# Neighbourhood attention: the product with the values as one fp32 product instead of three fp32r products

## Chip, cores and metric

The kernel runs on one core of one Trainium2 chip. The metric is the time of one execution on the device in microseconds (us). Three runs of the kernel before gave 3692.43 us as their median, with 3691.71 and 3695.13 as their ends.

## The reference

The program is a two-layer backbone over 1024 latent tokens with 256 context tokens. The second layer runs a latent attention (C) and beside it a two-dimensional neighbourhood attention (D). The change touches only D: 8 heads of width 64, the latents seen as 16 rows of 64 columns. A query sees 8 rows of keys around its own and in each of them 16 columns around its own column, with a learned bias, and all 256 context tokens.

```
def row_block(args):
    r, qr = args
    rs = jnp.clip(r - kr // 2, 0, rows - kr)
    krows = lax.dynamic_slice_in_dim(kg, rs, kr, axis=1).reshape(B, kr * GRID_W, H, d)
    ...
    kk = jnp.concatenate([krows, kc], axis=1)
    vv = jnp.concatenate([vrows, vc], axis=1)
    return mha_attend(qr, kk, vv, bias, mask)

def mha_attend(q, k, v, bias=None, mask=None):
    ...
    p = jax.nn.softmax(s, axis=-1)
    return jnp.einsum('bhqk,bkhd->bqhd', p.astype(v.dtype), v)
```

All of it is float32. The last line, exponentials times values, is what is computed in another way.

## The kernel before

`trunk` issues the stages one after the other, each a block of five instruction streams with its own semaphores. `attend` (L1855) is one function for three stages: "ab" (window attention, layer 0, 405 to 601 us of the trace), "ac" (latent attention, layer 1) and "ad" (neighbourhood attention, layer 1, about 2605 to 2846 us). After "ad" comes `layer_end`, which reads what "ad" stored.

Tiling. A query tile is 128 tokens and so is a key tile. Four query tiles are a block. `steps_of_head` lists for one head, block by block, the key tiles that any query tile of the block sees: 16 steps a head. A step works on one key tile and the 1 to 4 neighbouring query tiles that see it, so it is 128 to 512 columns wide. The widths of a head's steps are, in order: 512 (context), 384, 512, 512, 512, 256, 128, 512 (context), and for the second block 512 (context), 128, 256, 512, 512, 512, 384, 512 (context). Two heads make a pair of 32 steps, and `walk` runs four pairs, the middle ones in a loop.

One step x, engine by engine:
- TensorE (PE), `score` (L2111): keys times queries into one of three PSUM banks (L2129), bias added as two products with the identity (L2131), the row of maxima brought in by a last product of 65 rows (L2134, which waits for `row` on a block's first step).
- ScalarE (ACT), `exps` (L2211): with `split`, the exponential twice, once as float32 (`pt_sb`, L2217) and once rounded to fp32r (`ph`, L2218); without, once (L2220).
- VectorE (DVE), `low_part` (L2327): `pl` = `pt_sb` - `ph` (L2331), only with `split`.
- PE, `values` (L2136): the product with the values of an earlier step, x - LAG, accumulated over a block into one PSUM bank (L2151).
- At a block's end ACT copies the sums (`take_sums`, L2222) at the step LAG after the block's last, PE transposes them (`turn`, L2155) at the step after that, and DVE divides by the total (`result`, L2305). The first product with values of the next block waits for that copy.

Once a head, with `split`, ACT makes `vh` from the values (L2203) and DVE `vl` (L2325). Between the steps PE also computes rough scores for the coming block (`rough`, L2086: L2097 and L2100), DVE takes their maxima (L2293) and builds a diagonal of them (L2297), and PE spreads these over all rows (`extreme`, L2103: L2108), from which ACT makes the row (`extreme_row`, L2194: L2199). SyncE (SP) loads the next pair's queries, keys and values in `fetch` (L2040), after `s.pv` says that the last product of that head and pair is done (L2047).

The order on each engine is fixed by x alone. Two numbers of it hang on `split`:

```
PT, LAG = 4, 3 if split else 2
...
if split:
    pe.wait_ge(s.lo, nth(i, x))
    ...
else:
    pe.wait_ge(s.ex, nth(i, x))
...
prods = ((vh, ph), (vl, ph), (vh, pl)) if split else ((v_sb, pt_sb),)
for y, (v, e) in enumerate(prods):
    mm = pe.matmul(k.ps[0:v_width + 1, OB, (t.q - q0) * P:(t.q - q0 + t.n) * P], v[:, p, t.key],
                   e[:, x % PT, 0:t.n * P], start=(t.first and y == 0), stop=(t.last and y == len(prods) - 1))
```

The stage "ab" is called with `split` false; "ac" and "ad" with `split` true. The arrays `v_sb` and `pt_sb` are float32, the four split ones fp32r.

Of the kernel before, what the change touches and what calls it, by code (L numbers as in the profile page):

```python
# [33 lines left out]
HD = 64  # L34
# [210 lines left out]
def next_free(nc):  # L245

    return -(-nc.sbuf_base // 32) * 32
# [1552 lines left out]
def window_pieces():  # L1800

    out = []
    for q in range(LT):
        lo, hi = max(0, q - 1), min(LT, q + 2)
        masks = ([(0, CTX)] if q > 0 else []) + ([(1, CTX + (q + 1 - lo) * P)] if q < LT - 1 else [])
        out.append(Piece(q, [(SEQ, CTX), (lo * P, (hi - lo) * P)], masks=masks))
    return out + [Piece(q, [(SEQ, CTX)]) for q in range(LT, NT)]


def neighbour_pieces():  # L1810

    out = []
    for q in range(LT):
        rows = [min(max(r - NA_ROWS // 2, 0), 2 * LT - NA_ROWS) for r in (2 * q, 2 * q + 1)]
        n = rows[1] - rows[0] + NA_ROWS
        n += n % 2

        out.append(Piece(q, [(SEQ, CTX), (rows[0] * GRID_W, n * GRID_W)],
                         bias=(rows[0] - 2 * q + NA_ROWS - 1, n, rows[1] > rows[0])))
    return out  # L1820
# [549 lines left out]
def stacked_loader(qk, q_base, k_index, v_dram, v_index, v_width, n_q):  # L2370

    def load(sp, i, p, places, near, far):
        if sp is None:
            return 3, 3
        q_sb, k_sb, v_sb, q_top, k_top = places
        h, kh, vh = i * 2 + p, k_index(i, p), v_index(i, p)
        if q_sb is not None:
            keys(sp, h, kh, q_sb, k_sb, q_top, k_top, near, far)
        if v_sb is not None:
            sp.dma_start(v_sb, v_dram.rearrange("(t p) d -> p t d", p=P)[:, :, bass.ds(vh * v_width, v_width)]).then_inc(far, 16)  # L2380

    def keys(sp, h, kh, q_sb, k_sb, q_top, k_top, near, far):
        one = lambda x: qk[bass.ds(x, 1)].squeeze(0)
        sp.dma_start(f32(q_sb[:, 0, 0:n_q]), one(h + q_base)[:, 0:n_q]).then_inc(near, 16)
        for half in range(2):
            sp.dma_start(f32(k_sb[half * HD:(half + 1) * HD, 0]), one(kh)[0:HD]).then_inc(near, 16)
        sp.dma_start(f32(q_top[:, 0:n_q]), one(h + q_base)[0:HD, 0:n_q]).then_inc(far, 16)
        sp.dma_start(f32(k_top), one(kh)[HD:2 * HD]).then_inc(far, 16)
    return load


def parts_loader(k):

    def load(sp, i, p, places, near, far):
        if sp is None:
            return 2, 3
        q_sb, k_sb, v_sb, _, _ = places
        h = i * 2 + p
        one = lambda x: k.qkC[bass.ds(x, 1)].squeeze(0)
        for part, sem in enumerate((near, far)):  # L2400
            sp.dma_start(f32(q_sb[0:MLA_QK, part, 0:SEQ]), one(h)[part, :, 0:SEQ]).then_inc(sem, 16)
            sp.dma_start(f32(k_sb[0:MLA_QK, part]), one(h + MLA_HEADS)[part]).then_inc(sem, 16)
        sp.dma_start(v_sb, k.vC.rearrange("(t p) d -> p t d", p=P)[:, :, bass.ds(h * MLA_V, MLA_V)]).then_inc(far, 16)
    return load


def bias_loader(k):


    def load(sp, i, p, place, placeT, sem):  # L2410
        first_row = (i * 2 + p) * RPB_R + 1
        for q in range(2):
            sp.dma_start(place[q * GRID_W:(q + 1) * GRID_W],
                         k.bias[:, bass.ds(first_row - q, 2 * NA_ROWS - 2)]).then_inc(sem, 16)
            for key in range(2):
                first = 1 + q - key
                rows = k.biasT[:, first:first + 2 * NA_ROWS - 2].rearrange("k (d two) h c -> k d two h c", two=2)[:, :, 0]
                sp.dma_start(placeT[key * GRID_W:(key + 1) * GRID_W, :, q * GRID_W:(q + 1) * GRID_W],
                             rows[:, :, bass.ds(i * 2 + p, 1)].squeeze(2)).then_inc(sem, 16)
    return load  # L2420
# [965 lines left out]
def trunk(nc, out, **ins):  # L3386
    with ExitStack() as st:
        k = Core(nc, st, ins, out)
        ev = ins["ev_w_in"][0]
        load_b = stacked_loader(k.qkB, 0, lambda i, p: 8 + i // 2, k.vB, lambda i, p: i // 2, HD, TOK)  # L3390
        load_d = stacked_loader(k.qkD, 0, lambda i, p: i * 2 + p + 8, k.vD, lambda i, p: i * 2 + p, HD, SEQ)
        ahead_b = HeadAhead(k, st, "hb", SBUF_END, load_b, ins["wtab"], sink=ins["swa_sink"][0])
        ahead_a = DiffAhead(k, st, "ha", ahead_b.end)
        rows_0, rows_1 = RowsAhead(k, st, "h0", 0, KT // 2), RowsAhead(k, st, "h1", 1, 0)
        ahead_d = HeadAhead(k, st, "hd", SBUF_END, load_d, ins["ntab"], bias=bias_loader(k))
        units_b = [Unit(512, 512, 8, ins["swa_q_g"][0], HD ** -0.5, True, k.qkB, 0),
                   Unit(1024, 256, 2, ins["swa_k_g"][0], 1.0, True, k.qkB, 8, v=128, v_dst=k.vB),
                   Unit(0, 512, v=512, v_dst=k.vA)]
        made_b = ProjectionAhead(k, "pb", 1280, units_b, 2)
        opening(k, ev, 1024, made_b)  # L3400
        start_a = ProjectionStart(k, st, "pa", 0, ev, 0, made_b.raw_at, made_b.h_at)
        stores_b = project(k, "pb", 0, ev, 1024, 1280, units_b, keeps_h=True, vectors=(2, 3), made=made_b, begins=start_a)
        stores_a = project(k, "pa", 0, ev, 0, 1024, [
            Unit(0, 512, 8, ins["diff_q_g"][0], HD ** -0.5, True, k.qkA, 0),
            Unit(512, 512, 8, ins["diff_k_g"][0], 1.0, True, k.qkA, 8)], keeps_h=False, ahead_of=ahead_b, vectors=(4, 5),
            begun=start_a, stores_before=stores_b)
        ahead_d.hold_biases(st, rows_1.offset)
        stores_ab = attend(k, "ab", window_pieces(), 8,
               load_b,
               "two", False, HD, k.mix[0], 512, sink=ins["swa_sink"][0], beside=BiasSpread(k, ins["na_rpb"][0]),  # L3410
               ahead=ahead_b, ahead_of=ahead_a, last_stores=stores_a[0], stores_before=stores_a[1], keys_of=ahead_a)
        o_at = next_free(k.nc) + 100 * 1024
        stores_aa = attend_diff(k, "aa", ins, ahead_a, rows_0, stores_ab, o_at)
        layer_end(k, "e0", 0, TOK, [(0, 512), (512, 512), (1024, 256)], ins["w_out"][0], ins["mlp_w1"][0], ins["mlp_w2"][0], rows_0, stores_aa,
                  subln=ins["diff_subln_g"][0], following=ins["ada_w"][1])
        od = ins["od_w_in"][0]
        weights_end = next_free(k.nc) + 8 * KT * 1536
        start_c = LowRankStart(k, st, "pc", 1, od, next_free(k.nc), weights_end, weights_end + 8 * RAW_SLOTS * 256 + 4 * KT * P)
        stores_d = project(k, "pd", 1, od, MLA_QL + MLA_KVL + MLA_ROPE, 1536, [
            Unit(0, 512, 8, ins["na_q_g"][0], HD ** -0.5, False, k.qkD, 0, latents=True),  # L3420
            Unit(512, 512, 8, ins["na_k_g"][0], 1.0, False, k.qkD, 8),
            Unit(1024, 512, v=512, v_dst=k.vD)], keeps_h=True, sums_at=NEXT_BANKS, begins=start_c)
        project_low_rank(k, "pc", 1, od,
            Rank(0, MLA_QL, 0, ins["mla_qa_g"][0], ins["mla_wq_up"][0], ins["mla_q_g"][0], MLA_QK ** -0.5, 0, False),
            Rank(MLA_QL, MLA_KVL, MLA_ROPE, ins["mla_kva_g"][0], ins["mla_wkv_up"][0], ins["mla_k_g"][0], 1.0,
                 MLA_HEADS, True), start_c, stores_d)
        stores_ac = attend(k, "ac", [Piece(q, [(0, TOK)]) for q in range(LT)], MLA_HEADS, parts_loader(k), "three", True, MLA_V, k.mix[1], 0,
                           ahead_of=ahead_d, builds=ahead_d)
        stores_ad = attend(k, "ad", neighbour_pieces(), NA_HEADS,
               load_d,  # L3430
               "two", True, HD, k.mix[1], 512, bias=bias_loader(k), ahead=ahead_d, rows_of=rows_1, stores_before=stores_ac,
               o_at=next_free(k.nc) + 84 * 1024)
        layer_end(k, "e1", 1, SEQ, [(0, 512), (512, 512)], ins["w_out"][1], ins["mlp_w1"][1], ins["mlp_w2"][1], rows_1, stores_ad)
        k.phases.end()
# [21 lines left out]
```

## Time and profile before

| | |
|---|---|
| median of three runs | 3692.43 us (3691.71 to 3695.13) |
| the profiled execution, its own time | 3693.51 us |
| its span, first to last instruction | 3691.7 us |
| TensorE busy | 94% of the span |
| VectorE busy | 59% |
| ScalarE busy | 36% |
| mean granted TensorE clock | 0.969 |

The profile is of one execution. A matmul's end is modelled, so a drawn record reaches into the next one; the distance between two starts is the pace. "PEld" is TensorE's loading of weights, which runs ahead of the products. The idle time of an engine that nothing waits for costs nothing.

### The profile page before, as it was taken

What the parts mean: (1) busy time and instruction counts of PE and PEld (TensorE: products, weight loads), DVE (VectorE), ACT (ScalarE), POOL (GpSimd) and SP (SyncE); (2) the same over time, 40 slices, a digit from 0 to 9 for tenths busy, and PEclk for the clock granted to TensorE, in tenths of its full rate; (3) what the DMA queues carried; (4) which work ended last, traced back from release to release, by engine and by line L of the source; (5) the groups of instructions that cost most, each with busy time, mean ns of one, the idle gap of its engine ahead of it and who ended that gap; (6) DMA issues with size and microseconds to landing.
All of it is one profiled execution on the core that took longest, in us unless ns stands there. A gap on an engine that the chain in (4) does not pass through costs nothing. (4 is left out here: it accounts for less than half of the span.)

```text
span 3691.7 us, 47952 instructions
## 1 busy us (share of the span) xinstructions
PE 3479.7 (94%) x17598; PEld 2838.9 (77%) x17598; DVE 2171.4 (59%) x3199; ACT 1333.0 (36%) x2429; POOL 190.8 (5%) x197
## 2 busy tenths in 40 slices
PE   7999898998999999999989997899999999999998
PEld 4878666886888888888868786676787778888887
DVE  5879666886755444554475554788686553333333
ACT  5543344664511111111145554566565421111111
POOL 1110300000300000000001001000000110000000
PEclk8999899999999999999989998899999999999999
DMA  6566565324322212222233544233454311111112
GB/s 237 196 223 215 133 136 137 78 57 133 92 73 65 65 52 71 67 69 61 62 119 129 196 141 135 61 72 88 85 113 96 109 40 52 50 47 51 51 46 69
DMA packets 433093, 366.45 MB, mean 99 GB/s; under 512 B 104469, under 2 KB 375077, under 8 KB 427813
## 3 DMA queue, kind: packets, MB, share of 16 engines
q1 hardware_dynamic: 432933, 364.36, 34.9%
q8 instruction: 96, 1.57, 0.2%
q14 instruction: 64, 0.52, 0.1%
HBM read 276.60 MB, written 87.69 MB: 99 GB/s over the span
## 5 line engine op out<-in xcount | busy, mean ns | idle before, releaser
L2687 DVE SCALAR_TENSOR_TENSOR xT<-ps,mods,xT 128x1024 f32<-128x1024 f32 (+1 forms) x190 | 187.8, 1016 | 352.5 <-PE ps L2928 352.5
L3287 DVE TENSOR_TENSOR e_plain<-e_plain 128x1280 f32<-128x1280 f32 (+1 forms) x64 | 86.9, 1358 | 482.2 <-ACT e_plain L3126 482.2
L2928 PE MATMUL ps<-e_gh,e_w2h 128*128 128x512 f32 x1280 | 352.1, 372 | 6.0 <-DVE e_w2l L3225 3.7
L2928 PE MATMUL ps<-e_gh,e_w2l 128*128 128x512 f32 x1280 | 349.1, 370 | 0.0
L2928 PE MATMUL ps<-e_gl,e_w2h 128*128 128x512 f32 x1280 | 349.0, 370 | 0.0
L3126 ACT ACTIVATE e_plain<-ps 128x1280 f32<-128x1280 f32 (+1 forms) x64 | 72.7, 1135 | 722.7 <-PE ps L2928 718.6
L2928 PE MATMUL ps<-e_hh,e_w1l 128*128 128x512 f32 (+1 forms) x1200 | 327.2, 370 | 0.0
L2928 PE MATMUL ps<-e_hl,e_w1h 128*128 128x512 f32 (+1 forms) x1200 | 327.2, 370 | 0.0
L2928 PE MATMUL ps<-e_hh,e_w1h 128*128 128x512 f32 (+1 forms) x1200 | 327.1, 370 | 0.0
L2928 PEld LDWEIGHTS ps<-e_gh,e_w2h 128*128 128x128 f32 x1280 | 222.4, 188 | 55.1 <-DVE e_gl L3291 8.0
L3074 ACT CAST e_w2h<-e_raw 128x512 fp32r<-128x512 f32 x128 | 79.3, 620 | 499.4 <-PE ps L2928 499.4
L2928 PEld LDWEIGHTS ps<-e_gh,e_w2l 128*128 128x128 f32 x1280 | 223.5, 188 | 42.9
L2928 PEld LDWEIGHTS ps<-e_gl,e_w2h 128*128 128x128 f32 x1280 | 223.6, 188 | 42.6
L2928 PEld LDWEIGHTS ps<-e_hh,e_w1l 128*128 128x128 f32 x1200 | 209.6, 188 | 40.1
L2928 PEld LDWEIGHTS ps<-e_hh,e_w1h 128*128 128x128 f32 x1200 | 209.7, 188 | 39.8
L2928 PEld LDWEIGHTS ps<-e_hl,e_w1h 128*128 128x128 f32 x1200 | 209.6, 188 | 39.9
L2883 PE MATMUL ps<-e_hh,e_w1h 128*128 128x512 f32 (+1 forms) x320 | 125.3, 392 | 20.3 <-DVE e_w1l L3191 17.3
L2331 DVE TENSOR_TENSOR ac_pl<-ac_pt,ac_ph 128x512 fp32r<-128x512 f32 x160 | 112.4, 716 | 45.7 <-ACT ac_ph L2218 42.5
L2217 ACT ACTIVATE ac_pt<-ps 128x512 f32<-128x512 f32 x160 | 95.9, 599 | 85.0 <-PE ps L2134 84.8
L2883 PE MATMUL ps<-e_hl,e_w1h 128*128 128x512 f32 (+1 forms) x320 | 121.2, 379 | 0.0
L2883 PE MATMUL ps<-e_hh,e_w1l 128*128 128x512 f32 (+1 forms) x320 | 121.2, 379 | 0.0
L2640 DVE TENSOR_REDUCE aa_nm<-ps 128x1 f32<-128x1280 f32 (+1 forms) x80 | 102.0, 1276 | 27.8 <-PE ps L2543 25.4
(436 smaller groups left out, 7555.6 us busy)
## 6 DMA issues: line engine op xcount, KB each, us to landing
e_raw<-in_mlp_w SPq DMA_DIRECT2D x64, 512.0 KB, 4.2
e_raw<-in_mlp_w SPq DMA_DIRECT2D x128, 256.0 KB, 3.0
rstd<-in_ada_w SPq DMA_DIRECT2D x64, 384.0 KB, 3.4
e_raw<-in_w_out SPq DMA_DIRECT2D x40, 512.0 KB, 3.9
qkC<-pc_stage SPq DMA_DIRECT2D x72, 192.0 KB, 2.7
hT<-pb_hb SPq DMA_DIRECT2D x10, 1024.0 KB, 6.0
pa_hb<-hT SPq DMA_DIRECT2D x10, 1024.0 KB, 6.8
qkA<-pa_stage SPq DMA_DIRECT2D x20, 512.0 KB, 3.6
```

Source lines behind the costliest of these rows:

```text
L2217: nc.scalar.activation(pt_sb[:, x % PT, 0:t.n * P], scores(x)[:, 0:t.n * P], ACT.Exp).then_inc(s.pf, 1)
L2331: nc.vector.tensor_tensor(pl[:, x % PT, 0:n], pt_sb[:, x % PT, 0:n], f32(ph[:, x % PT, 0:n]), ALU.subtract).then_inc(s.lo, 1)
L2640: nc.vector.tensor_reduce(negmax[:, v % 2, m:m + 1], scores(m)[:, 0:pieces[v % NQ].width], AX.X, ALU.max, negate=True).then_inc(s.mx, 1)
L2687: ins = k.nc.vector.scalar_tensor_tensor(out=x, in0=ps, scalar=k.mods[:, layer, gate, bass.ds(n, 1), w], in1=x, op0=ALU.mult, op1=ALU.add)
L2883: mm = pe.matmul(part_sums(u), wt[:, u % 2, f], o[:, f, c0:c0 + w], start=(not begun and f == fs[0] and x == 0), stop=(fs is not early_f a ...
L2928: mm = pe.matmul(k.ps[:, SB * (e % 2) + b, 0:n], w[:, e % 2, f], m[:, f, c0:c0 + n], start=(f == 0 and x == 0), stop=(f == nf - 1 and x == 2))
L3074: nc.scalar.copy(wh[:, e % 2], raw[:, e % 2, 0:nf]).then_inc(s.whi, 1)
L3126: nc.scalar.activation(plain[:, e], k.ps[:, SB * (e % 2):SB * (e % 2) + SB].rearrange("p b c -> p (b c)")[:, 0:n_tok], ACT.Relu).then_inc( ...
L3287: nc.vector.tensor_tensor(g, g, g, ALU.mult).then_inc(s.sqg, 1)
```

## The change

One argument of one call: `split` is false in the call of `attend` for the neighbourhood attention. By it the exponentials are computed once, nothing is split into a high and a low part, each step has one float32 product in place of three fp32r products, and `LAG` is 2 instead of 3.

```
@@ -3428,7 +3428,7 @@
                            ahead_of=ahead_d, builds=ahead_d)
         stores_ad = attend(k, "ad", neighbour_pieces(), NA_HEADS,
                load_d,
-               "two", True, HD, k.mix[1], 512, bias=bias_loader(k), ahead=ahead_d, rows_of=rows_1, stores_before=stores_ac,
+               "two", False, HD, k.mix[1], 512, bias=bias_loader(k), ahead=ahead_d, rows_of=rows_1, stores_before=stores_ac,
                o_at=next_free(k.nc) + 84 * 1024)
```

## Rows read from the trace of the kernel before

**Rows 1.** The page: busy us of each engine, share of span, instructions

```profile
PE 3479.7 (94%) x17598; PEld 2838.9 (77%) x17598; DVE 2171.4 (59%) x3199; ACT 1333.0 (36%) x2429; POOL 190.8 (5%) x197
```

**Rows 2.** Busy time in 2619:2844: length, PE, PEld, DVE, ACT, POOL, clock, DMA, GB/s

```profile
2619.00:2844.00 225.00, 221.46 (x1324) 180.61 (x1323) 181.28 (x314) 138.95 (x296) 0.00 (x0) 0.99 0.47 99
```

**Rows 3.** Waits of PEld, 2619:2844: who, for whom, us in total, times, longest

```profile
PEld ps L2134 <- ACT hd_qe L2199: 2.9, 8, 1.0
PEld ps L2134 <- ACT ad_qe L2199: 2.7, 8, 1.0
PEld ps L2097 <- DVE ad_nm L2293: 1.9, 5, 1.1
PEld ps L2097 <- DMA ad_k<-qkD: 1.6, 1, 1.6
PEld ps L2097 <- issue: 1.4, 2, 0.9
PEld ps L2151 <- DVE ad_pl L2331: 0.4, 1, 0.4
```

**Rows 4.** Groups of instructions, 2619:2844, DVE and ACT: busy us, mean ns, idle before

```profile
L2331 DVE TENSOR_TENSOR ad_pl<-ad_pt,ad_ph 128x512 fp32r<-128x512 f32 (+3 forms) x128 | 73.2, 586 | 18.0 <-ACT ad_ph L2218 17.3 <-issue 0.2
...
L2218 ACT ACTIVATE ad_ph<-ps 128x512 fp32r<-128x512 f32 (+3 forms) x128 | 66.0, 515 | 0.0
L2227 ACT COPY ad_oT<-ps 65x512 f32<-65x512 f32 x16 | 9.3, 581 | 2.3 <-PE ps L2151 1.7
```

**Rows 5.** Line 2151: durations ns min/median/max, first and last start, forms

```profile
L2151 PE MATMUL ps<-ab_pt,ab_v x256: 270/442/1057, 411.3 to 599.3; 128*65 128x256 f32 x48, 128*65 128x512 f32 x32, 128*65 128x384 f32 x32, 128*65 128x128 f32 x16
...
L2151 PE MATMUL ps<-ad_ph,ad_vh x128: 221/391/442, 2625.9 to 2843.0; 128*65 128x512 f32 x80, 128*65 128x384 f32 x16, 128*65 128x256 f32 x16, 128*65 128x128 f32 x16
```

**Rows 6.** Timeline of PE, 2703:2704: start us, length us, instruction

```profile
2703.01 0.39 PE L2151 MATMUL ps<-ad_ph,ad_vh 128*65 128x512 f32 x1
2703.24 0.39 PE L2151 MATMUL ps<-ad_ph,ad_vl 128*65 128x512 f32 x1
...
2703.70 0.39 PE L2129 MATMUL ps<-ad_q,ad_k 128*128 128x512 f32 x1
```

**Rows 7.** Timeline of PE: three triples, first start and next instruction

```profile
2706.66 0.33 PE L2151 MATMUL ps<-ad_ph,ad_vh 128*65 128x384 f32 x1
...
2707.18 0.40 PE L2129 MATMUL ps<-ad_q,ad_k 128*128 128x512 f32 x1
...
2838.60 0.28 PE L2151 MATMUL ps<-ad_ph,ad_vh 128*65 128x256 f32 x1
...
2838.95 0.33 PE L2129 MATMUL ps<-ad_q,ad_k 128*128 128x384 f32 x1
...
2640.87 0.23 PE L2151 MATMUL ps<-ad_ph,ad_vh 128*65 128x128 f32 x1
...
2641.06 0.44 PE L2129 MATMUL ps<-hd_q,hd_k 128*128 128x512 f32 x1
```

**Rows 8.** Timeline of PE, window attention: one 512-wide product of fp32, and what follows

```profile
471.77 1.02 PE L2151 MATMUL ps<-ab_pt,ab_v 128*65 128x512 f32 x2
472.23 0.74 PE L2129 MATMUL ps<-hb_q,hb_k 128*128 128x384 f32 x1
472.81 0.34 PE L2131 MATMUL ps<-ab_wb,identr_sb 128*128 128x384 f32 x1
```

**Rows 9.** Timeline of PE, window attention: fp32 products of the other widths

```profile
476.90 0.81 PE L2151 MATMUL ps<-ab_pt,ab_v 128*65 128x384 f32 x2
...
475.03 0.60 PE L2151 MATMUL ps<-ab_pt,ab_v 128*65 128x256 f32 x2
...
473.46 0.38 PE L2151 MATMUL ps<-ab_pt,ab_v 128*65 128x128 f32 x2
```

**Rows 10.** Waits of PE, 2619:2844

```profile
PE ps L2097 <- DMA ad_k<-qkD: 1.8, 2, 1.1
```

**Rows 11.** Waits of PE in the window attention, 405:601

```profile
PE ps L2160 <- ACT ab_oT L2227: 3.3, 15, 0.3
```

## What I predict, and why

> **What bounds the kernel now.** I read the page first: TensorE (PE) is busy 94% of the span [rows 1]. An average over stages says little about one stage, so the second view is the table of busy time over the stretch in which the changed call (`attend` named "ad") works at its steady pace: 225.00 us, of which PE is busy 221.46, VectorE (DVE) 181.28 and ScalarE (ACT) 138.95, at a granted clock of 0.99 of the upper level, 2.4 GHz [rows 2]. What is left of PE is 3.5 us. The third view, the waits of the weight loads (PEld) in the same stretch, shows which other engines PE waits for: six kinds, 25 waits, 10.9 us in all [rows 3]. A weight load may start up to one product (0.23 us) ahead of its own product, so these waits overstate the loss: 10.9 - 25 x 0.23 is about 5 us. Between 3.5 and 10.9 us of waiting is all that this stage has. It is a stage bound by the work that PE is given, and the change alters that work.
>
> **What the change removes.** With `split` false, each of the 128 value steps loses the second exponential `ph` on ACT (66.0 us in all) and the subtraction `pl` on DVE (73.2 us) [rows 4]. The eight pairs of `vh` and `vl` go too. Both engines had room: ACT 86 us of 225, DVE 44 us [rows 2]. The product with the values waited for `pl` once, 0.4 us [rows 3]. So the removed work is nearly all beside PE and is worth only the waits that it causes.
>
> **What it does to the product.** Three fp32r products of a step become one fp32 product. The same stage has 128 steps: 80 of 512 columns and 16 each of 384, 256 and 128 [rows 5]. The price of the new form is in this trace, because the window attention (`attend` named "ab", 405 to 601 us) already multiplies unsplit fp32 exponentials and values by the same line, with the same 128 x 65 weights. Its 128 products leave 256 records [rows 5]: one fp32 product is two records.
>
> Before, 512 columns: starts at 2703.01 and 2703.24, and the instruction after the third at 2703.70, so three take 0.69 us; a record is drawn 0.39 long, that is 0.16 longer than its pace [rows 6]. The other widths, by the same differences from first start to the next instruction: 384 takes 0.52, 256 takes 0.35, 128 takes 0.19 us [rows 7].
>
> After, 512 columns: the two records of one product are together 1.02 us, less the drawn tail of 0.16 leaves 0.86. A second reading: the product starts at 471.77, one 384-wide product follows (0.17 at its pace), the one after it starts at 472.81, so 0.87 [rows 8]. I take 0.86. The other widths the same way: 384 is 0.81 - 0.16 = 0.65, 256 is 0.44, 128 is 0.22 us [rows 9].
>
> The differences: 80 x 0.17 = 13.6; 16 x 0.13 = 2.1; 16 x 0.09 = 1.4; 16 x 0.03 = 0.5. PE gets **17.6 us more work** in a stage where it has 5 us to spare. The form, the weights and the widths are those of the trace, so the uncertainty here is some 0.01 us a step, 1.3 us.
>
> **What it gives back.** `split` false also sets `LAG` to 2: the product of step x-2, not x-3, is issued after the scores of step x, and all else that hangs on products comes a step earlier.
> - PE waits 1.8 us for the DMA of the next pair's keys, in two waits [rows 10]. `fetch` holds those loads until the last product of the pair, which now comes one step (225/128 = 1.8 us) earlier relative to the scores that need them: I take 1.8 back.
> - The wait for `pl` at the end, 0.4, goes [rows 3].
> - The rough scores wait for DVE's maxima: 1.9 us in 5 waits of the weight load, about 0.8 after the cover of 5 x 0.23, and "issue" 1.4 us in 2, about 0.9 [rows 3]. DVE loses 80 of its 181 us; I take 0.8 and half of 0.9 back. It could be nothing or all.
> - The first scores of a block wait for ACT's row of maxima (`row`), 2.9 + 2.7 us in 16 waits, 1.9 after cover [rows 3]. ACT is free earlier now. But between `extreme` (L2108) and that wait stands a product with values, and at steps 7 and 23 of a pair it was a 512-wide one of 0.69 us and will be, one step later in the list, a 256-wide one of 0.44. The gain and the loss are alike; I count nothing, with 1.9 either way in the range.
> Together 1.8 + 0.4 + 0.8 + 0.5 = **3.5 us back**.
>
> **A wait that it adds.** `turn` transposes the sums of a block as soon as ACT has copied them (`take_sums`, 0.58 us [rows 4]), `LAG` + 1 steps after the block's last. In between PE has the scores of one step. At `LAG` 3 these are 512 wide (at steps 3, 11, 19 and 27 of a pair), about 1 us. At `LAG` 2 they are those of steps 2, 10, 18 and 26; at 10 and 26 they are 256 wide, about 0.55 us. So in 8 places of the stage the copy is late. What is queued behind the waiting transpose is the whole of PE's queue: the products with values of the next block, then the next scores. The window attention, at `LAG` 2 with short steps, shows the price: 3.3 us in 15 waits, 0.22 each [rows 11]. 8 x 0.22 = **1.8 us**.
>
> Edits with one answer: the buffers `vh`, `vl`, `ph`, `pl` leave, the output stays at its fixed place, and what follows starts from the same semaphores, so nothing moves after the stage but by its delay. No DMA is added. The clock stays at its upper level: it is at 0.99 here with PE idle 3.5 us of 225 [rows 2], and PE will be idle no more. At the end of the stage three triples become two fp32 products, both on PE's path and in the sum above.
>
> **The sum.** 17.6 - 3.5 + 1.8 = 15.9 us. Against the profiled execution of 3693.5 us that is 3709.4; the median of the three runs is 1.1 lower, so **3708.3 us**, 0.43% slower. What a measurement of this kernel can tell from no change is about 0.2%, or 7.4 us, so the bound to slower is at 3699.8.
>
> **The rivals.**
> (a) The relief is worth more. If ACT and DVE cause all waits that the weight loads show, 10.9 us come back and none is added: 17.6 - 10.9 = 6.7, so 3699.1, within 0.2%. It needs over 10.2 us back. Against it: PE's own idle time is 3.5 us [rows 2], and most of the 10.9 lies under running products. Chance 0.08.
> (b) The other side: one fp32 product is cheaper than three. If PE streamed it at half rate, once, 512 columns would take 0.43 us, the length between the starts of two records; the other widths 0.32, 0.22, 0.11. Against the triples that is 80 x 0.26 + 16 x (0.20 + 0.13 + 0.08) = 27 us less, so 3665 us. It decides by the number of records per product: with one, faster; with two, slower. 256 records for 128 products [rows 5] and 1.02 us for a pair [rows 8] speak against it. Chance 0.03.
> The Trainium skill bears on this in two places. "Perfetto Trace Analysis", Engine Utilization, halves the array's output rate for a form that it calls FP32_LOW_HIGH, and read alone it gives (b). "FP8 and Floating Point Precision", TensorE Precision Notes, says that true FP32 takes four passes, against one of the reduced form; four against three would add a third of 72 us (80 x 0.69 + 16 x (0.52 + 0.35 + 0.19)), less what the triples lose between their products. The trace agrees with both at once: each record runs at half rate, and there are two.
> (c) The shorter lag costs more. If nothing is given back and each of the 16 blocks waits 0.22 us: 17.6 + 3.5 = 21.1, so 3713.5. Or the product with values, at its lag of two, waits for its own exponential; against that speaks that two steps are 3.5 us and the exponential takes 0.5 [rows 4]. Chance 0.12 for 3711 and above.
> The forecast has 0.77.
>
> **How the numbers follow.** The forecast's own range is 15.9 with 1.3 for the price, and 3 on either side for the waits: 3704 to 3712. To leave out no more than 2 in 10 I stretch it to 3701 and 3713. Slower by over 0.2%: 0.77 + 0.12 = 0.89; within 0.2%: 0.08; faster: 0.03.
>
> **What would show it.** Line 2151 should leave 256 records of `ad_pt,ad_v`, some 1.02 us for a 512-wide pair; the stretch should grow from 225 to about 241 us with PE's idle time near 3 us; DVE should be busy about 101 us and ACT 67; waits for the DMA of the keys should be gone, and new ones of L2160 for `ad_oT` should appear, eight or so. The stages before and after should keep their length. It is wrong if the pairs take less than 0.80 us, if the stage's waits shrink by over 10 us, or if another stage moves by more than 2 us.

## The result, and the profile after

The changed kernel takes 3707.85 us (median of seven runs, 3703.67 to 3710.42) against 3693.82 us of the kernel before (seven runs, 3691.71 to 3697.57). The ratio is 1.0039, with a 95% interval of 1.0028 to 1.0050: slower, by about 14 us. The prediction was 3708.3 us. One execution in all that follows, of the kernel before with LAG 2, ran slow (5405.02 us at a granted clock of 0.587) and is in no median, ratio or profile here.

The page of the changed kernel gives busy us of each engine, share of the span and instructions (before: [rows 1]):

```profile
span 3708.7 us, 47349 instructions
PE 3502.3 (94%) x17470; PEld 2832.6 (76%) x17470; DVE 2100.0 (57%) x3063; ACT 1281.1 (35%) x2293; POOL 192.6 (5%) x197
```

PE has gained 22.6 us of drawn busy time with 128 records fewer, DVE has lost 71 and ACT 52. To read the stage itself, take its length from the first L2134 to the transpose behind the last product, in the timeline of PE. The kernel before:

```profile
2619.59 0.79 PE L2134 MATMUL ps<-hd_qe,hd_ke 65*128 65x512 f32 x1 [0.29 <-ACT hd_qe L2199]
...
2844.54 0.28 PE L2160 MATMUL ps<-ident_sb,ad_oT 65*128 65x65 f32 x1 [0.67 <-ACT ad_oT L2227]
```

and the changed one:

```profile
2621.18 0.79 PE L2134 MATMUL ps<-hd_qe,hd_ke 65*128 65x512 f32 x1 [0.24 <-ACT hd_qe L2199]
...
2862.13 0.34 PE L2160 MATMUL ps<-ident_sb,ad_oT 65*128 65x65 f32 x2 [0.67 <-ACT ad_oT L2227]
```

So 224.95 us became 240.95: **16.0 us more, all in this stage**. The rest of the span, 3691.7 - 225.0 = 3466.7 and 3708.7 - 241.0 = 3467.7, moved by 1. The parts of that rest move more than their sum: the window attention, whose code is untouched, took 204.7 us in the profile before and 207.2 in this one. The table of busy time over the stretch (length, PE, PEld, DVE, ACT, POOL, clock, DMA share, GB/s), after [rows 2] the line to compare:

```profile
2621.00:2862.00 241.00, 238.69 (x1195) 169.22 (x1195) 111.95 (x178) 84.20 (x160) 0.00 (x0) 0.99 0.42 91
```

PE is idle 2.3 us of 241, at the same granted clock of 0.99. DVE and ACT have more room than ever, and nobody needs it.

The product itself. Line 2151 over the whole kernel (durations in ns, first and last start), and one step of the timeline of PE (start, length):

```profile
L2151 PE MATMUL ps<-ad_pt,ad_v x256: 270/590/596, 2626.8 to 2860.9; 128*65 128x512 f32 x80, 128*65 128x384 f32 x16, 128*65 128x256 f32 x16, 128*65 128x128 f32 x16
```

```profile
2707.44 1.02 PE L2151 MATMUL ps<-ad_pt,ad_v 128*65 128x512 f32 x2
2707.89 0.74 PE L2129 MATMUL ps<-hd_q,hd_k 128*128 128x384 f32 x1
2708.47 0.52 PE L2131 MATMUL ps<-hd_bT,identr_sb 128*128 128x384 f32 x2
```

Two records of together 1.02 us for 512 columns, as in the window attention [rows 8]. From 2707.44 to 2708.47 less 0.17 for the 384-wide product between is 0.86 us, against 0.69 for three fp32r products [rows 6]. Summed over all 128 steps, each record counted at the distance between two starts inside a product, the products took 72.2 us before and 89.9 after: **17.7 us**; the sum predicted 17.6. Counted instead from a product's first start to what follows it (0.697 and 0.859 us as medians for 512 columns), they took 72.8 and 89.5, so 16.7. The price is known to about 1 us.

The waits of the weight loads (who, for whom, us in total, times, longest), to compare with [rows 3]; "issue" rows are left out, for they come to 42 us in a stage where PE itself is idle 2.3, so nearly all of it lies under running products:

```profile
PEld ps L2134 <- ACT hd_qe L2199: 3.5, 8, 1.0
PEld ps L2134 <- ACT ad_qe L2199: 3.1, 8, 0.8
PEld ps L2160 <- ACT ad_oT L2227: 2.6, 8, 0.4
PEld ps L2129 <- ACT ad_pt L2220: 1.5, 8, 0.2
```

The waits for the DMA of the keys, for DVE's maxima and for `pl` are gone. New are eight waits of the transpose for `ad_oT`, at steps 10 and 26 of each pair. One of them in the timeline of PE:

```profile
2700.47 0.33 PE L2134 MATMUL ps<-hd_qe,hd_ke 65*128 65x256 f32 x1
2700.98 0.47 PE L2160 MATMUL ps<-ident_sb,ad_oT 65*128 65x65 f32 x4 [0.17 <-ACT ad_oT L2227]
```

The 256-wide product needs 0.12 us, so the transpose could have started at 2700.59; it waited 0.39, of which the drawn tail hides all but 0.17.

So everything that the prediction named was there. But a sum of three terms can be right with two of them wrong, and the experiments show that it was.

### The profile page after: what moved, and what is told of

The parts are those of the page before. It is cut to its first block and busy times, and to the rows that moved or that the text cites. A ratio compares the mean times of both kernels' runs of the same rounds, so it can differ in the third digit from the quotient of the medians.

```text
span 3708.7 us, 47349 instructions
## 1 busy us (share of the span) xinstructions
PE 3502.3 (94%) x17470; PEld 2832.6 (76%) x17470; DVE 2100.0 (57%) x3063; ACT 1281.1 (35%) x2293; POOL 192.6 (5%) x197
## 5 line engine op out<-in xcount | busy, mean ns | idle before, releaser
L2928 PEld LDWEIGHTS ps<-e_gl,e_w2h 128*128 128x128 f32 x1280 | 223.4, 188 | 42.8
L2293 DVE TENSOR_REDUCE ad_nm<-ps 128x1 f32<-128x768 f32 (+1 forms) x64 | 65.6, 1025 | 111.1 <-PE ps L2100 111.0
```

The costliest lines, as they stand in the source:

```text
L2293: nc.vector.tensor_reduce(m, here, AX.X, ALU.max, negate=True).then_inc(s.top, 1)
L2928: mm = pe.matmul(k.ps[:, SB * (e % 2) + b, 0:n], w[:, e % 2, f], m[:, f, c0:c0 + n], start=(f == 0 and x == 0), stop=(f == nf - 1 and x == 2))
```

## Experiments

All lengths below are of the stage as just defined, from one profiled execution each. Where a kernel leaves the stage untouched it came out at 224.95, 225.34 and 223.37 us, so a difference below 2 us isn't told apart. Nearly all of that spread is one kind of wait, that of PE for the DMA of the keys (both `ad_k` and `hd_k`): it was 2.3, 2.4 and 0.7 us in these three, and without it the stage comes out at 222.7, 222.9 and 222.7. The table gives that wait for each kernel; its product's share goes by the distances inside a product. Times of whole kernels spread by some 4 to 8 us to either side of their median; the kernel before had medians of 3691.74, 3690.63 and 3691.41 us beside these runs, and each ratio is against its own.

| kernel | stage, us | product's share | waits for the keys' DMA | ratio to before (95%) |
| --- | --- | --- | --- | --- |
| before (three fp32r, split work, LAG 3) | 224.95 | 72.2 | 2.3 |  |
| fp32 product alone | 237.48 | 89.9 | 0.8 | 1.0026 (1.0015 to 1.0037) |
| fp32 product, no split work, LAG 3 | 235.86 | 89.9 | 0 | 1.0025 (1.0016 to 1.0034) |
| the change: the same with LAG 2 | 240.95 | 89.9 | 0 | 1.0039 (1.0028 to 1.0050) |
| the change, two rough scores later | 237.84 | 89.9 | 0 | 1.0029 (1.0018 to 1.0040) |
| the same, and the maxima spread first | 236.01 | 89.9 | 0 | 1.0031 (1.0021 to 1.0042) |
| relief alone | 222.76 | 72.2 | 1.6 | 0.9993 (0.9984 to 1.0002) |
| before with LAG 2 | 233.81 | 72.2 | 0 | 1.0021 (1.0011 to 1.0032) |
| two of three products | 211.31 | 48.2 | 1.6 | 0.9957 (0.9943 to 0.9971) |
| before, the maxima spread first | 224.95 | 72.2 | 0 | 0.9998 (0.9989 to 1.0007) |

**The product alone.** The kernel before, with the split work done and waited for, but one fp32 product:

```
-prods = ((vh, ph), (vl, ph), (vh, pl)) if split else ((v_sb, pt_sb),)
+prods = ((vh, ph), (vl, ph), (vh, pl)) if split and name != "ad" else ((v_sb, pt_sb),)
```

> The kernel before, with one edit in the neighbourhood attention: the product with the values is one fp32 product of v and pt; the second exponential, pl, vh and vl are still computed and waited for, and LAG stays 3. Stage length here and below is from the first L2134 of the stage to its last L2160 group: 224.95 us before, 240.95 after. My theory (the stage is PE's work, and the fp32 product is 17.7 us dearer): stage 242.6 us, time 3711.5 us. Relief rival (ACT and DVE set several us of waits, the freed engines gave them back in the changed kernel, so the product must cost well over 17.7 us to end at +14): the stage is 245 us or more, since nothing is relieved here. Half-rate rival: below 224 us.

Measured: stage 237.5 us, median 3702.25. The products cost their 17.7 (or 16.7), but the stage grew by 12.5 only. So some 4 to 5 us came back **with ACT and DVE as loaded as before** and at LAG 3. The stretch, to compare with [rows 2], and the waits of PE in it:

```profile
2620.00:2857.00 237.00, 235.21 (x1195) 168.09 (x1194) 181.00 (x312) 139.18 (x295) 0.00 (x0) 0.99 0.44 93
```

```profile
PE ps L2097 <- DMA hd_k<-qkD: 0.5, 1, 0.5
PE ps L2134 <- ACT ad_qe L2199: 0.5, 1, 0.5
PE ps L2097 <- DMA ad_k<-qkD: 0.3, 1, 0.3
PE ps L2134 <- ACT hd_qe L2199: 0.3, 1, 0.3
```

The waits for the DMA of the keys are 0.8 us, where they were 2.3 (the 1.8 of [rows 10] and one of 0.5 for `hd_k`), without the loads being issued a step earlier. A slower PE comes later and may find them there; but the untouched stage showed 0.7 us as well, so this fall alone proves nothing. Without these waits the stage grew from 222.7 to 236.7, by 14.0, and 3.7 us (2.7 by the other count) still came back: the weight loads' waits for DVE's maxima, 1.9 us in [rows 3], are gone from this kernel's list though DVE has the same work. My theory of the price held and that of the waits fell. The relief rival fell too, since nothing was relieved here.

**LAG 3 in the changed kernel.**

```
-PT, LAG = 4, 3 if split else 2
+PT, LAG = 4, 3 if split or name == "ad" else 2
```

> The changed kernel with LAG 3 in place of 2 in the neighbourhood attention, so fp32 product and no split work, but the old order. Theory: against the run with the split work kept it saves only the waits for pl and for DVE's maxima, about 1.7 us: stage 241 us, time 3709.8; the waits of L2160 for ad_oT at steps 10 and 26 are gone (they were 2.7 us in 8 places), the waits for the DMA of the keys are back (1.8 us). So LAG itself is worth under 1 us either way. Relief rival: 4 us or more below the run with the split work kept. Lag rival: LAG 3 is 3 us or more better than LAG 2, stage 238 or less.

Measured: stage 235.9 us, median 3701.30. Against the run before it 1.6 us less, which is about what the expectation says and within what can't be told apart. But against the changed kernel it is **5.1 us less**: the lag rival, not my theory, was right. From the starts in the timeline, the changed kernel waits 2.7 us more between L2134 and L2160 (8 places) and 1.7 us more between L2129 and L2134 (1.84 against 0.13), and 0.5 more among the transposes themselves; with LAG 3 the transposes don't wait, but for the last of the stage, which waits in every kernel. Both kernels have the DMA waits at zero (my theory had them back with LAG 3), so with this product the earlier loads that I had credited to LAG 2 gave nothing.

**Two rough scores later.** Two lines of the list of places, for the neighbourhood attention alone:

```
     place[u] = min(first_step[b] - 3, following - max(1, NS // NQ))
+place = [y + (name == "ad" and u in (1, 9)) for u, y in enumerate(place)]
```

> The changed kernel with two of the 16 rough scores of a pair issued one step later (units 1 and 9, at steps 26 and 10), so that they stand between the scores of these two steps and the transpose of the block's sums. Theory: the transposes wait for ACT's copy because only 256-wide scores stand in between (2.7 us in 8 places of the stage); 0.5 us of work moved into each gap takes these waits away: stage 238.3 us, time 3705.2. Rival (the wait is one for PE's own products to drain, or the maxima come late instead): stage stays at 241, or a wait of L2097 for ad_nm appears of the same size.

Measured: stage 237.8 us, 3.1 less than the changed kernel, as the theory says (238.3), and no wait for the maxima in its place. The transposes waited because only a 256-wide score stood between them and the copy. The median, 3702.20, agrees with it, though the intervals of the two ratios overlap.

**The same, with the maxima spread first.** In PE's list of a step, for the neighbourhood attention:

```
-rough(i + n, u, True)      # all of the step's, then
-extreme(i + n, b, True)
+extreme(i + n, b, True)    # first
+rough(i + n, u, True)
```

> The changed kernel, LAG 2, with the two rough scores a step later as before and with PE issuing the spread of the maxima (L2108) ahead of the rough score of its step instead of behind it, so that the rough score covers ACT's copy of the row. Theory (the rest of what LAG 2 costs is the wait of a block's first scores for the row, since a 256-wide product stands ahead of it at steps 7 and 23): the waits between L2129 and L2134, 1.8 us in 8 places, are gone, stage 235.5 us (it was 237.8 with the rough scores moved alone, 235.9 with LAG 3), time 2 to 3 us below that run. Rival (they wait for something else on ACT): stage stays at 238.

Measured: stage 236.0 us (the theory said 235.5), another 1.8 less. By itself that is under the 2 us that can be told; the waits carry it. Of the 1.83 us of waits between L2129 and L2134 in 8 places, one of 0.56 is left. With both cures LAG 2 is as good as LAG 3 (235.9). So of the 5.1 us of LAG 2, 4.9 were these two waits: the copy of a block's sums (3.1) and the row of maxima (1.8). The median, 3701.52, isn't told from the one before it; here only the stage speaks.

**LAG 2 in the kernel before.**

```
-PT, LAG = 4, 3 if split else 2
+PT, LAG = 4, 3 if split and name != "ad" else 2
```

> The kernel before with LAG 2 in place of 3 in the neighbourhood attention, all else the same. In the fp32 pair of runs the step from LAG 3 to 2 made the stage 5.1 us longer (2.7 of it at the transposes, 1.7 at the first scores of a block). Theory (these waits come from the order alone, whatever the product): stage 5 to 8 us longer here too, 230 to 233 us, time 5 to 8 us above before, with waits of L2160 for ad_oT at steps 10 and 26, and more of L2134 for the row. My prediction's reading (LAG 2 gives back 1.8 us at the DMA of the keys and costs 1.8 at the transposes) says 225.

Measured: stage 233.8 us, 8.9 more than at LAG 3, a little over the upper end of what the theory said, and far from the 225 of my prediction's reading; median 3699.5, ratio 1.0021. The waits of the weight loads from 2619 to 2843, 10 us short of the stage's end:

```profile
PEld ps L2134 <- ACT hd_qe L2199: 4.3, 8, 1.0
PEld ps L2134 <- ACT ad_qe L2199: 4.2, 8, 1.3
PEld ps L2160 <- ACT ad_oT L2227: 2.6, 8, 0.4
PEld ps L2097 <- DVE ad_nm L2293: 2.5, 6, 0.6
PEld ps L2151 <- DVE ad_pl L2331: 2.2, 8, 0.4
```

The eight waits for `ad_oT` are the same 2.6 us as in the changed kernel, whatever the product. Here ACT has two exponentials a step ahead of the row of maxima, so those waits are larger (8.5 against 6.6), and the product waits for `pl` (3.5 us in ten waits over the whole stage, where it was 0.4 in one). There is no wait for the keys' DMA here, which is what I had credited to LAG 2; but neither is there one in a kernel below that keeps LAG 3, so it can't be put down to the lag. The shorter lag costs more with the split work (8.9 us) than without it (5.1).

**Relief alone.** Three fp32r products, but no float32 exponential and no `pl`; the third product takes `ph` again. Of the edit, the product's line (ACT's and DVE's lines and the wait for `pl` go with it):

```
-prods = ((vh, ph), (vl, ph), (vh, pl)) if split else ((v_sb, pt_sb),)
+prods = ((vh, ph), (vl, ph), (vh, ph if name == "ad" else pl)) if split else ((v_sb, pt_sb),)
```

> The kernel before, LAG 3 and three fp32r products a step in the neighbourhood attention, but without the float32 exponential and without pl: the third product takes ph a second time, so the low part of the exponentials is missing from the result. ACT loses 66 us and DVE 73 us, PE keeps all its work. It is the relief of the change without its dearer product. Stage length (first L2134 to last L2160 group) before 224.95 us. Theory as it stands after the first four runs (PE's work sets the stage, and the waits for DVE and the DMA shrink when DVE is freed or PE slowed): the waits go as they did with the fp32 product, stage 219 to 221 us, time 4 to 6 us below before. Rival (the relief is worth nothing, only the slower product took the waits away): stage 224 or more.

Measured: stage 222.8 us, 2.2 less; median 3690.08, ratio 0.9993 with 1 inside its interval. Neither my 219 to 221 nor the rival's 224 or more. DVE fell to 116.67 us and ACT to 88.82 in 222, yet the waits for the keys stayed at 1.6 us:

```profile
2620.00:2842.00 222.00, 220.06 (x1323) 180.66 (x1323) 116.67 (x185) 88.82 (x167) 0.00 (x0) 0.99 0.46 99
```

```profile
PE ps L2097 <- DMA ad_k<-qkD: 1.2, 1, 1.2
PE ps L2097 <- DMA hd_k<-qkD: 0.4, 1, 0.4
PE ps L2134 <- ACT hd_qe L2199: 0.3, 1, 0.3
```

Freeing DVE of 65 us and ACT of 50 was worth 2.2 us at most, just above what can be told, and 1.5 with the waits for the keys left out (222.7 against 221.2).

**Two of three products.**

```
-prods = ((vh, ph), (vl, ph), (vh, pl)) if split else ((v_sb, pt_sb),)
+prods = (((vh, ph), (vh, pl)) if name == "ad" else ((vh, ph), (vl, ph), (vh, pl))) if split else ((v_sb, pt_sb),)
```

> The kernel before with the product of vl and ph left out in the neighbourhood attention: that part of the sum is missing, all else is issued as before. Theory (PE's work sets the time one for one): 128 products fewer, 80 x 0.23 + 16 x (0.175 + 0.12 + 0.06) = 24 us, less up to 3 us of new waits for DVE, which is busy 181 us of the 201 then left: stage 201 to 204 us, time 3670 to 3673. Rival (a chain through ACT and DVE is the next bound close behind PE): the stage falls by under 15 us, to 210 or more.

Measured: stage 211.3 us, 13.6 less, while the products took 24.0 less; median 3677.16, ratio 0.9957. The rival of a second bound close behind was the better one. The stretch and its weight loads' waits:

```profile
2620.00:2831.00 211.00, 202.94 (x1195) 164.66 (x1195) 180.22 (x313) 136.09 (x296) 0.00 (x0) 0.99 0.50 105
```

```profile
PEld ps L2097 <- DVE ad_nm L2293: 8.9, 15, 0.9
PEld ps L2134 <- ACT hd_qe L2199: 4.3, 8, 1.0
PEld ps L2134 <- ACT ad_qe L2199: 4.2, 8, 1.3
```

PE is now idle 8 us, 3.9 of them in waits for DVE's maxima, and its weight loads wait 8.9 us for these maxima (1.9 in [rows 3]); DVE is busy 180 of 211. So the stage doesn't follow PE's work one for one in either direction: of 17.7 us more, 12.5 arrive (71%; 75% of 16.7); of 24.0 us less, 13.6 (57%).

**The maxima spread first, in the kernel before.** The order of the cure above, with split work and LAG 3.

> The kernel before with one edit in the neighbourhood attention: PE issues the spread of the maxima (L2108) ahead of the rough score of its step. Theory (a block's first scores wait for ACT's row because too little of PE's work stands between): 1.3 us of waits between L2129 and L2134 go, stage 223.5 to 224.3 us against 224.95, and the time is not told from before. Rival (the rough score, now later, makes DVE's maxima late): the waits of L2097 grow by as much, stage 225 or more.

Measured: stage 224.95 us, no change to the hundredth, median 3691.33, ratio 0.9998. The rival named the outcome (225 or more), though not the wait: that of L2097 for the maxima is 1.9 us as before. The waits of the weight loads from 2619 to 2843; the stage here runs from 2616.6 to 2841.6, so the `hd_qe` row lacks the first wait of 1.0 us, and the `ad_oT` row lies at the stage's end and behind it:

```profile
PEld ps L2108 <- DVE ad_diag L2297: 2.9, 6, 0.5
PEld ps L2097 <- DVE ad_nm L2293: 1.9, 9, 0.5
PEld ps L2134 <- ACT ad_qe L2199: 1.9, 6, 1.0
PEld ps L2160 <- ACT ad_oT L2227: 1.3, 2, 1.2
PEld ps L2134 <- ACT hd_qe L2199: 1.0, 4, 0.4
```

Over the whole stage the waits for the row shrank from 5.6 us to 3.9, and 2.9 us of waits of L2108 for DVE's diagonal came. PE has no wait for the keys' DMA in this execution, against 2.3 before. Without that wait the stage is 224.95 against 222.7, and the last experiment below, with the same order here, has 226.4 with 1.7 us of that wait, so 224.7. By these two the edit rather cost 2 us, hidden in this execution by a DMA that was in time. The same edit was worth 1.8 us where DVE had 112 us of work in 241 and nothing where it had 181 in 225: the spread needs DVE's diagonal, and here the busier DVE delivers it late.

**The mirror in the window attention.** If PE is what counts, the opposite change should pay where the kernel has the dear form: three fp32r products in "ab".

```
-       "two", False, HD, k.mix[0], 512, sink=ins["swa_sink"][0], ...
+       "two", True, HD, k.mix[0], 512, sink=ins["swa_sink"][0], ...
```

> The kernel before with the mirror of the change in the window attention (ab): three fp32r products of split exponentials and values in place of one fp32 product, LAG 3, with pl laid over pt and one table of the bias laid where the next stage's tiles come later, to make room. The stage from its first rough score to its last transpose is 204.7 us before. PE loses 32 x 0.17 + 32 x 0.12 + 48 x 0.08 + 16 x 0.04 = 13.8 us, DVE gains about 69 us and goes from 114 to 183 of 196 us. Theory (what PE loses comes back in part only, as 13.6 of 24 us did when one of three products was left out with DVE as busy): stage 196 to 200 us, time 5 to 9 us below before. Rival one (PE's work counts in full): stage 191. Rival two (DVE becomes the bound): no gain, stage 204 or more.

The edit also holds the loading of the next stage's tables until those of the bias have landed.

Measured: 3715.44 us, ratio 1.0068 (1.0054 to 1.0082). The stage went from 204.7 to 226.8 us. My theory had the sign wrong. Of the rivals the second had the direction, but not its cause, since DVE idles a fifth of the time. Busy times over 405 to 630, which reaches 9 us behind the stage, and three of the longest waits between 405 and 601:

```profile
405.00:630.00 225.00, 181.03 (x1120) 144.66 (x1120) 178.30 (x465) 133.38 (x337) 31.96 (x48) 0.95 0.56 120
```

```profile
PEld ps L2097 <- DVE ab_top L2287: 30.4, 31, 1.5
DVE ab_pl L2331 <- ACT ab_ph L2218: 26.7, 15, 4.2
PE ps L2097 <- DVE ab_top L2287: 21.1, 30, 1.3
```

Up to the stage's end at 621, PE is idle 40 of 216 us and DVE 42. DVE works through one list: `pl` stands ahead of the maxima, waits there for ACT's second exponential (26.7 us), and the maxima behind it are what PE's next rough scores wait for (21.1 us, where it was 0.3 between 405 and 601 before). Neither engine is full; by these waits the order ties them together. That is read from the waits, and no run takes the order alone apart. This run moved the lag, the tiles and the product at once, so how much of the 22 us is the lag's isn't known from it; but the lag alone is the next run.

**LAG 3 in the window attention, one fp32 product.**

```
-PT, LAG = 4, 3 if split else 2
+PT, LAG = 4, 3
```

> The kernel before with LAG 3 in the window attention (ab), where it was 2; the product stays one fp32 product. Length from its first rough score to its last transpose: 204.7 us before, 203 to 207 in other kernels that did not touch it. Theory (what LAG 2 cost in the neighbourhood attention, 5.1 us with fp32 products, it costs here too: PE waits 3.3 us for ad-like copies of sums and 3.6 for rows): 198 to 201 us, time 3 to 6 us below before. Rival (in ab DVE's chain of maxima sets the pace, since PE has 12 us idle of 196): 203 or more, no gain.

Measured: its stage 202.8 us against 204.7 (203 to 207 where it was untouched), median 3691.52, ratio 0.9997 (0.9988 to 1.0007). Between theory and rival, and no gain that can be told. The waits of PE, 400 to 606, first lines:

```profile
PE ps L2097 <- DVE ab_top L2287: 5.4, 15, 0.9
PE ps L2543 <- PEq L2037: 1.7, 1, 1.7
PE ps L2108 <- DVE ab_diag L2297: 1.5, 1, 1.5
PE ps L2134 <- ACT hb_qe L2199: 1.3, 7, 0.2
```

The 3.3 us for `ab_oT` [rows 11] are gone from the list, and the waits for DVE's maxima have grown from 2.1 to 5.4. With one fp32 product the lag is worth no loss, so the 22 us of the mirror aren't those of the lag by itself.

**Both, in all three stages.** LAG 3 and the maxima spread first everywhere.

> LAG 3 in the window attention and, in all three stages that attend makes, the spread of the maxima ahead of the rough score. Theory: the rest of the row waits in the window attention goes as well, 2 us more than with LAG 3 alone, ab at 196 to 199 us, the neighbourhood attention as in the run with the spread first alone; time 5 to 9 us below before, which would beat both kernels. Rival: DVE gets the rough scores later and the gain is lost, ab as with LAG 3 alone or longer.

Measured: window attention 201.8 us where the theory said 196 to 199, neighbourhood attention 226.4, median 3688.59, ratio 0.9996 (0.9987 to 1.0005). Not told from before. No kernel here that computes everything is shown faster than the kernel before.

## Why the prediction was right, and where it was right by luck

- **The bound.** PE's work sets the stage: right. At equal order and equal load of the others 12.5 us of the 17.7 that were added to it arrived in the stage, and relieving ACT and DVE alone gave 2.2 us at most.
- **The price of the product.** 17.6 us predicted, 17.7 measured by the same kind of reading, 16.7 up to the start of what follows a product. Taking the form, weights and widths from a stage that already used them is why. The Trainium skill ("FP8 and Floating Point Precision", TensorE Precision Notes) counts four passes for true FP32. It gives no count for the reduced form; that it is one pass was my reading. The trace fits the four if each of the two records is two passes, but the ratio isn't four to three: 0.86 to 0.69 us is 1.25, since each fp32r product of 512 columns takes 0.23 us and half of an fp32 record 0.216 (starts 0.431 apart, halved).
- **What it gives back.** 3.5 us predicted. Measured at LAG 3, where nothing of the order changes: 5.2 from the slower PE (4.2 with the price at 16.7; 1.5 of either are waits for the keys' DMA) and 1.6 from the relief, less than can be told by itself, together 6.8 (or 5.8). The step that failed is the cause. I took 1.8 us of waits for the DMA as a gift of the earlier loads at LAG 2; with the fp32 product these waits are gone at LAG 3 too. They are also the one term that changes from execution to execution (0.7 to 2.4 us in the untouched stage), so a reading of 1.8 in one profile was no price; and I had left out the 0.5 for `hd_k`. The waits for DVE's maxima, which I had put down to the relief, went with DVE as loaded as before. I had not seen that waits for other engines shrink by themselves when the bound engine gets more work.
- **The wait it adds.** 1.8 us in 8 places predicted; 2.7 us in exactly these 8 places measured, and the step from LAG 3 to 2 costs 5.1 in all. I named the second cause, the row of maxima at steps 7 and 23, and counted it as a draw with the freed ACT. It was a loss of 1.7 to 1.8 us against LAG 3.
- **The sum.** Predicted 17.6 - 3.5 + 1.8 = 15.9; measured 17.7 - 6.8 + 5.1 = 16.0. Both corrections were too small by 3.3 us, and the two errors cancelled: that is luck. With the price at 16.7 it is 16.7 - 5.8 + 5.1, and the errors are 0.9, 2.3 and 3.3. The 16.0 is the difference of two profiled executions; the medians differ by 14.0, with 10 to 18 as the interval, so the agreement to a tenth is luck as well.
- **What would show it.** The stage at 241 us, 256 records, the eight waits, no wait for the keys: all found. DVE was busy 112 us, not 101, and ACT 84, not 67: consecutive records of one engine overlap in the drawing (two exponentials of 0.60 us start 0.49 apart), so the 66.0 and 73.2 us of the removed groups [rows 4] were not all busy time of their own. One sign of being wrong came up and means nothing: another stage, the window attention, moved by 2.5 us. It was 203.2 to 207.2 us in ten profiles of kernels that leave it alone, so 2 us was too tight a bound.
- **The rivals.** (a), more relief: no. (b), half rate: no. (c), the dearer lag: its mechanism was real, and its price, 5.1, was above the 3.5 that I gave it; only the larger give-back kept the time inside.

## What to carry to other kernels

Dropping a split to spare the side engines is a loss when the product's engine is the bound: one fp32 product costs 1.25 times three fp32r products here. Count the price of the bound engine's work from a stage that already has the form, and then expect waits for others to take up a part: here they absorbed some 30% of what was added, and grew by nearly half of what was taken away. A wait for a DMA that one profile shows may be absent from the next execution of the same code; compare several before it enters a sum. A flag that also changes the order of issue is two changes; time them apart. Here the order cost 5.1 us of 16, and most of that could be undone by moving two scores and one spread.

## What the runs showed that was not expected

The pace of a product of 512 columns is 0.232 us as fp32r and 0.216 us for half a record as fp32, both at a granted clock of 0.99 of 2.4 GHz. In the mirror, a stage whose three engines were busy 82%, 81% and 61% of 216 us was 22 us longer than one with PE at 94%: by the waits, a queue in program order on DVE set it, not the load of any engine. No run tests that by changing the order alone. In the neighbourhood attention with its code untouched, the stage took 223.4 us in one execution and 225.3 in another, and the waits for the keys' DMA, 0.7 and 2.4 us, differ by as much.
